# A decoder layer's recurrent sample outputs: from TensorE products with the new state to VectorE sums over a transposed copy of the old state

## The reference

```
S_new = diag(e) S + k^T v        (256 x 512, returned as gla_state_sample)
o     = q S_new                  (512 numbers, goes on into a norm and the branch)
```

## Time and profile before

| | us |
|---|---|
| runs, median of 3 | 5105.1 |
| lowest, highest | 5100.22, 5108.11 |
| profiled execution, its own time | 5101.16 |
| its span, first to last instruction | 5099.3 |
| blocks with units, with TensorE's work alone | 506.15 to 930.45 |
| the 32 blocks after them | 930.45 to 1295.81 |

### The profile page before, as it was taken

The page is one execution under the profiler, slowest core; times in us unless marked ns, Lnnn a source line. Parts: engine busy times, 40 slices in busy tenths (PEclk is TensorE's granted clock), DMA queues, the critical chain, the costliest instruction groups (busy, mean ns, idle before and its releaser), DMA issues.

```text
span 5099.3 us, 63408 instructions
## 1 busy us (share of the span) xinstructions
PE 4302.3 (84%) x24722; PEld 3722.8 (73%) x24722; DVE 3047.0 (60%) x4037; ACT 852.2 (17%) x1238; POOL 1266.2 (25%) x824
## 2 busy tenths in 40 slices
PE   5999999999688989999567568799999999677555
PEld 5998999999676889777456457688788878444222
DVE  5533222211542654675567887778889756698776
ACT  3434333222221233000110000000000000000000
POOL 0000000000000000233123433444434422266665
PEclk9999999999699899999688879899999999888777
DMA  5555555333245455999568879999999998699998
GB/s 178 194 204 179 200 192 206 134 113 113 73 176 218 141 190 192 424 423 420 204 238 363 325 312 411 411 423 423 423 392 400 424 405 354 252 401 382 422 421 362
DMA packets 312222, 1494.07 MB, mean 293 GB/s; under 512 B 34658, under 2 KB 119954, under 8 KB 147132
## 3 DMA queue, kind: packets, MB, share of 16 engines
q0 software_dynamic: 114288, 830.54, 39.6%
q1 hardware_dynamic: 197748, 661.07, 34.3%
HBM read 1411.79 MB, written 79.70 MB: 292 GB/s over the span
## 4 chain that ended last, share of the span: by engine, by line
PE 52%; DMA 26%; DVE 9%; issue 5%; DVEq 3%; POOL 2%; ACT 2%; SPq 0%; POOLq 0%; ACTq 0%
PE psum L501 27%; DMA sb_raw<-in_wstream 15%; PE psum L2500 10%; DMA sb_ring<-in_peer_v,sb_idx_all 8%; PE psum L555 6%; DVE sb_acc L2341 2%; POOL sb_ring L2315 2%; DMA sb_gt<-dram_z 2%; PE psum L2742 2%; DVE sb_acc_b L2643 1%; PE psum L716 1%; PE psum L2724 1%; DVE sb_split L485 1%; PE psum L1127 1%; DVEq L1678 1%
## 5 line engine op out<-in xcount | busy, mean ns | idle before, releaser
L501 PE MATMUL psum<-sb_actr,sb_split 128*128 128x264 f32 x8112 | 1014.3, 287 | 43.9 <-DVE sb_split L485 17.9
L485 DVE TENSOR_TENSOR sb_split<-sb_raw,sb_split 128x2048 fp32r<-128x2048 f32 x201 | 460.8, 2293 | 966.7 <-ACT sb_split L481 965.8
L501 PEld LDWEIGHTS psum<-sb_actr,sb_split 128*128 128x128 f32 x8112 | 1001.4, 191 | 47.6 <-issue 44.0
L2336 DVE CUSTOM_DVE_ANT_0 sb_ring<-sb_ring,sb_htok 128x2048 f32<-128x2048 f32 x264 | 598.3, 2291 | 204.3 <-DMA sb_ring<-in_peer_u,sb_idx_all 189.4
L2226 POOL DMA_INDIRECT sb_ring<-in_peer_u,sb_idx_all x256 | 374.9, 1465 | 1335.8 <-DVE sb_dots L2336 678.1
L2341 DVE SCALAR_TENSOR_TENSOR sb_acc<-sb_ring,sb_coef,sb_acc 128x2048 f32<-128x2048 f32 x256 | 601.9, 2351 | 141.1 <-DMA sb_ring<-in_peer_v,sb_idx_all 125.5
L2226 POOL DMA_INDIRECT sb_ring<-in_peer_v,sb_idx_all x256 | 417.8, 1632 | 664.1 <-DVE sb_acc L2341 556.3
L2742 PE MATMUL psum<-sb_ring,sb_diag 128*128 128x512 f32 x512 | 349.0, 845 | 238.5 <-DMA sb_ring<-in_peer_v,sb_idx_all 231.5
L2643 DVE SCALAR_TENSOR_TENSOR sb_acc_b<-sb_ring,sb_coef_b,sb_acc_b 128x2048 f32<-128x2048 f32 x192 | 451.4, 2351 | 131.0 <-DMA sb_ring<-in_peer_v,sb_idx_all 116.6
L2315 POOL DMA_INDIRECT sb_ring<-in_peer_v,sb_idx_all x256 | 436.5, 1705 | 299.3 <-DVE sb_acc_b L2643 131.5
L2500 PE MATMUL psum<-sb_h2b,sb_raw 128*128 128x256 f32 x2048 | 455.5, 382 | 18.5 <-DMA sb_raw<-in_wstream 18.5
(11 more groups left out here) (366 smaller groups left out, 4274.8 us busy)
## 6 DMA issues: line engine op xcount, KB each, us to landing
sb_raw<-in_wstream SPq DMA_DIRECT2D x386, 1024.0 KB
sb_raw_u<-in_wstream SPq DMA_DIRECT2D x64, 1024.0 KB
dram_z<-sb_zst SPq DMA_DIRECT2D x64, 260.0 KB
sb_states<-in_state SPq DMA_DIRECT2D x32, 512.0 KB, 3.4
out_gla_s<-sb_states SPq DMA_DIRECT2D x32, 512.0 KB, 2.9
sb_vrow<-dram_v SPq DMA_DIRECT2D x8, 1024.0 KB, 5.2
sb_cache<-in_kcache SPq DMA_DIRECT2D x8, 1024.0 KB, 11.5
sb_cache<-in_vcache SPq DMA_DIRECT2D x8, 1024.0 KB, 7.6
```

Source lines behind the costliest of these rows:

```text
L485: nc.vector.tensor_tensor(split[:, slot, 1, :], raw[:, slot, :], split[:, slot, 0, :], ALU.subtract).then_inc(lo_ready, 1)
L501: last = nc.tensor.matmul(psum[:, bank, 0:ntok], w[a], acts(b, kt), start=(i == 0 and a == 0 and b == 0), stop=(i == len(kts) - 1 and a == 1))
L2336: nc.vector.tensor_tensor_reduce(u[:], u[:], htok[:], 1.0, 0.0, ALU.mult, ALU.add, out).then_inc(row_used, 1)
```

## The change

The products of the new state with q are no longer computed. Instead the kernel takes `o = (q * e) S + (q . k) v`:

- A second input array holds each old state transposed, as 128 x 4 x 256 floats per unit (512 KB). SP loads it into one of two new buffers beside the state.
- VectorE does four fused multiply-and-sum operations per unit, each 128 x 256: a piece of the transposed old state times the row q * e, spread over all partitions, summed into one column (`dve_unit`). After a sample's last head it copies the 16 columns into `os_`.
- The rows q * e are made once: VectorE multiplies (`dve_samples_products`, at block N_R + 4), TensorE turns them and sums q * k over the partitions (`pe_samples_q`, at N_R + 8), ScalarE copies them out, SP stores them to DRAM and spreads sample 0's row; the row of the next sample is loaded with its value row.
- The term (q . k) v is made once for all (`dve_samples_own`) and added after the last unit (`dve_samples_done`).
- The units start 12 blocks later, at N_U0 = N_R + 12, and ride with the 32 blocks from there, 20 blocks before the stage ends. The 12 blocks before them are three segments of four.
- TensorE's loop in those blocks is now `seg_loop`, without `pe_unit`; ScalarE has no `act_unit_out`.
- Semaphores are merged and renamed (`v_tok` into `rows_tok`, `keep_made`, `peer_made`, `qm_zeroed` into `pool_made`, `packed` into `unpacked`), with counts adapted.

```diff
+N_U0 = N_R + 12
+N_UNITS = N_U0 + 4 * TS
...
         def sp_samples_start(sp):
 
-            sp.dma_start(states[0][:], state_of(ins["state"], 0, 0)).then_inc(st_in[0], 16)
-            sp.dma_start(states[1][:], state_of(ins["state"], 0, 1)).then_inc(st_in[1], 16)
-            sp.wait_ge(v_tok, 2)
+            for h in range(2):
+                sp.dma_start(states[h][:], state_of(ins["state"], 0, h)).then_inc(st_in[h], 16)
+                sp.dma_start(states_t[h][:], ins["stateT"][h]).then_inc(st_in[h], 16)
+            sp.wait_ge(rows_tok, 2)
...
+        def sp_samples_q(sp):
+
+            sp.wait_ge(rows_tok, 3)
+            sp.dma_start(q_dram[:], q8[:]).then_inc(samples_loaded, 16)
+            sp.wait_ge(samples_loaded, 80)
+            sp.dma_start(qrow[:], row_of(q_dram, 0)).then_inc(vrow_loaded, 16)
...
         def sp_unit(sp, n, s, h, last):
-            unit = n - N_R
+            unit = n - N_U0
             sp.wait_ge(st_done, unit + 1)
             sp.dma_start(state_of(outs["gla_s"], s, h), states[h % 2][:]).then_inc(st_out[h % 2], 16)
+            sp.wait_ge(st_read, unit + 1)
             if h == HEADS - 1 and not last:
-                sp.dma_start(vrow[:], row_of(s + 1)).then_inc(vrow_loaded, 16)
+                sp.dma_start(vrow[:], row_of(v_dram, s + 1)).then_inc(vrow_loaded, 16)
+                sp.dma_start(qrow[:], row_of(q_dram, s + 1)).then_inc(vrow_loaded, 16)
             if h < 2 or not last:
...
+                k = bass.ds(s * HEADS + (h + 2), 1)
+                sp.dma_start(states_t[h % 2][:], ins["stateT"][k].rearrange("a p j d -> p (a j) d")).then_inc(st_in[h % 2], 16)
+                src = ins["state"].rearrange("s h k v -> (s h) k v")[k].rearrange("a (k p) v -> p (a k) v", p=P)
                 sp.wait_ge(st_out[h % 2], s * 32 + 16 * (h // 2 + 1))
-                sp.wait_ge(st_read, unit + 1)
                 sp.dma_start(states[h % 2][:], src).then_inc(st_in[h % 2], 16)
...
+        def act_samples_q(act):
+            act.wait_ge(rows_turned, 3)
+            nc.scalar.activation(q8[:].rearrange("s (b f) -> s b f", b=2), psum[0:TS, 4:6, :], ACT.Copy).then_inc(rows_tok, 1)
...
-        def act_unit_out(act, n, s, h):
-            act.wait_ge(st_read, n - N_R + 1)
-            nc.scalar.activation(os_[:, 4 * h:4 * h + 4, bass.ds(s, 1)], psum[:, 4 + h % 2, 0:4].unsqueeze(2),
-                                 ACT.Copy).then_inc(os_read, 1)
...
+        def dve_samples_products(dve):
+
+            dve.wait_ge(es_ready, 1)
+            nc.vector.tensor_tensor(qes[:], qs[:], es[:], ALU.mult)
+            nc.vector.tensor_tensor(qks[:], qs[:], ks[:], ALU.mult)
+            dve.drain().then_inc(qes_ready, 1)
+
+        def dve_samples_own(dve):
+
+            dve.wait_ge(rows_turned, 3)
+            nc.vector.tensor_reduce(qk[:], psum[:, 6, 0:64].rearrange("p (h d s) -> p h s d", h=HEADS, d=2), AX.X, ALU.add)
+            dve.drain()
+            nc.vector.tensor_tensor(qkv[:].rearrange("p (h j) s -> p h j s", h=HEADS), vs[:].rearrange("p (h j) s -> p h j s", h=HEADS),
+                                    qk[:].unsqueeze(2).to_broadcast([P, HEADS, 4, TS]), ALU.mult)
+
+        def dve_samples_done(dve):
+            dve.drain()
+            nc.vector.tensor_tensor(os_[:], os_[:], qkv[:], ALU.add).then_inc(os_ready, 1)
...
             last.then_inc(st_done, 1)
+            dve.wait_ge(st_in[h % 2], s * 64 + 32 * (h // 2 + 1))
+            for j in range(4):
+                st = states_t[h % 2][:, j, :]
+                last = nc.vector.tensor_tensor_reduce(st, st, qrow[:, h * DK:(h + 1) * DK], 1.0, 0.0, ALU.mult, ALU.add,
+                                                      os_cur[:, 4 * h + j, :])
+            last.then_inc(st_read, 1)
+            if h == HEADS - 1:
+                dve.drain()
+                nc.vector.tensor_copy(os_[:, :, bass.ds(s, 1)], os_cur[:])
...
-        def pe_unit(pe, n, s, h):
-
-            pe.wait_ge(st_done, n - N_R + 1)
-            pe.wait_ge(os_read, n - N_R + 1)
-            for j in range(4):
-                for dt in range(2):
-                    last = nc.tensor.matmul(psum[:, 4 + h % 2, j:j + 1], states[h % 2][:, dt, j * P:(j + 1) * P],
-                                            qs[:, 2 * h + dt, bass.ds(s, 1)], start=(dt == 0), stop=(dt == 1))
-            last.then_inc(st_read, 1)
-
+        def pe_samples_q(pe):
+            pe.wait_ge(qes_ready, 1)
+            pe.wait_ge(rows_tok, 2)
+            for f in range(8):
+                nc.tensor.transpose(psum[0:TS, 4 + f // 4, (f % 4) * P:(f % 4 + 1) * P], qes[:, f, :], ident[:])
+            nc.tensor.matmul(psum[:, 6, 0:64], ones[:], qks[:].rearrange("p f s -> p (f s)"), start=True,
+                             stop=True).then_inc(rows_turned, 1)
...
         def act_gla(act, g):
             if g.samples:
+                act.wait_ge(os_ready, 1)
```

More of the change, by code:

```diff
@@ L69 @@
 N_END = N_WQ + 16
-N_UNITS = N_R + 4 * TS
+N_U0 = N_R + 12
+N_UNITS = N_U0 + 4 * TS
 N_UEND = N_END + NU
@@ L197, in mixer_kernel @@
         vrow = sb("vrow", [P, D], F32, R_M + 41472)
+        states_t = [sb(f"states_t{i}", [P, 4, DK], F32, R_M + 49664 + 4096 * i) for i in range(2)]
+        qrow = sb("qrow", [P, 1024], F32, R_M + 57856)
+        q8 = sb("q8", [TS, 1024], F32, R_M + 66048)
         v8 = sb("v8", [TS, D], F32, R_M + 86528)
@@ L208, in mixer_kernel @@
         low_s = sb("low_s", [RANK, TS], F32, R_SM + 2944)
+        qes = sb("qes", [P, 8, TS], F32, R_P + 66560)
+        qks = sb("qks", [P, 8, TS], F32, R_P + 66816)
+        qk = sb("qk", [P, HEADS, TS], F32, R_P + 67072)
+        qkv = sb("qkv", [P, KT, TS], F32, R_P + 67200)
+        os_cur = sb("os_cur", [P, KT, 1], F32, R_P + 67712)
         ks_cur = sb("ks_cur", [P, 8, 1], F32, R_SM + 2976)
@@ L414, in mixer_kernel @@
         vrow_loaded = sem("vrow_loaded")
-        os_read = sem("os_read")
+        es_ready = sem("es_ready")
+        qes_ready = sem("qes_ready")
+        os_ready = sem("os_ready")
         samples_loaded = sem("samples_loaded")
@@ L580, in unit_loop @@
         def unit_loop(eng, n0, n1, body):
-            assert (n0 - N_R) % 4 == 0 and (n1 - n0) % 4 == 0
+            assert (n0 - N_U0) % 4 == 0 and (n1 - n0) % 4 == 0
             with eng.Fori(0, (n1 - n0) // 4) as i:
@@ L585, in unit_loop @@
                     n = n0 + h
-                    body(i * 4 + n, n % 2, i * 2 + (n - n % 2) // 2, i + (n0 - N_R) // 4, h)
+                    body(i * 4 + n, n % 2, i * 2 + (n - n % 2) // 2, i + (n0 - N_U0) // 4, h)
         def with_units(n0):
-            return N_R <= n0 < N_UNITS
+            return N_U0 <= n0 < N_UNITS
         def sp_samples_first(sp):
@@ L642, in act_samples_start @@
                 if b == 1:
-                    last.then_inc(v_tok, 1)
-                    act.wait_ge(v_turned, 2)
-            last.then_inc(v_tok, 1)
+                    last.then_inc(rows_tok, 1)
+                    act.wait_ge(rows_turned, 2)
+            last.then_inc(rows_tok, 1)
             act.wait_ge(gx_ready, 2)
             nc.scalar.activation(es[:], gxs[:], ACT.Exp, scale=1.0 / GATE_NORM)
-            act.drain()
-            act.sem_inc(os_read, 2)
+            act.drain().then_inc(es_ready, 1)
+        def act_samples_q(act):
+            act.wait_ge(rows_turned, 3)
+            nc.scalar.activation(q8[:].rearrange("s (b f) -> s b f", b=2), psum[0:TS, 4:6, :], ACT.Copy).then_inc(rows_tok, 1)
         def act_unit(act, n, s, h):
-            unit = n - N_R
             if h == 0:
@@ L685, in dve_unit @@
                 dve.drain()
-                dve.wait_ge(vrow_loaded, s * 16 + 16)
-            dve.wait_ge(st_scaled, n - N_R + 1)
+                dve.wait_ge(vrow_loaded, s * 32 + 32)
+            dve.wait_ge(st_scaled, n - N_U0 + 1)
             for dt in range(2):
@@ L747, in sp_project @@
                     sp_samples_start(sp)
+                if n0 == N_R + 8:
+                    sp_samples_q(sp)
                 def body(n, slot, u, ntok=ntok):
@@ L804, in act_project @@
                     act_samples_start(act)
+                if n0 == N_R + 8:
+                    act_samples_q(act)
                 def body(n, slot, u, s=None, h=None, func=func, ntok=ntok, n0=n0):
@@ L921, in dve_project @@
                         dve_samples_first(dve)
+                    if n0 == N_R:
+                        dve_samples_start(dve)
+                    if n0 == N_R + 4:
+                        dve_samples_products(dve)
+                    if n0 == N_R + 8:
+                        dve_samples_own(dve)
+                    if n0 == N_UNITS:
+                        dve_samples_done(dve)
                     seg_loop(dve, n0, n1, lambda n, slot, u: split_lo(dve, n + 1, 1 - slot))
@@ L964, in pe_project @@
                     pe_samples_turn(pe, 0)
-                if with_units(n0):
-                    if n0 == N_R:
-                        pe_samples_turn(pe, 1)
-                        pe.wait_ge(act_lo, 9)
```

(20 more changed lines are left out.)

72 lines of the change are left out of this document (33 added, 39 removed).

## The result

| | before | after |
|---|---|---|
| median of the first set, 4 runs each | 5102.86 | 5043.81 |
| lowest, highest | 5100.22, 5108.11 | 5042.18, 5046.64 |
| profiled execution | 5101.16 | 5042.81 |
| its span | 5099.3 | 5041.1 |

The ratio is 0.9884, with a 95% interval of 0.9866 to 0.9901. The changed kernel is 59.05 us faster by these medians; 55.3 us was forecast. The same kernel in two later sets, each against the kernel before on the same chip, gave 0.9892 (0.9876 to 0.9909) and 0.9889 (0.9872 to 0.9905), which is 55.7 and 56.3 us.

What follows compares the result with a forecast made beforehand. TensorE's work was taken to bound the units' blocks. Removing 57.5 us and adding 2.2 gave -55.3, so 5105.1 became 5049.8, say 5050 us, with a range of 5044 to 5062.

Steps and rivals of the forecast that it cites:

- What bounds the kernel: Blocks N_R to N_UNITS - 1: TensorE's work sets the pace, 13.21 us a round, with the products on the path in full.
- Removed, 57.5 us: 32 units' rounds fall from 13.21 to 11.42 us; 53.8 if the extra 0.12 us a block stays.
- third rival: Products cheaper than their place in the chain, only 0.4 of 1.68 us truly theirs: gain 14.4, 5091 us; chance 0.01.
- Added on TensorE, 2.2 us: At N_R + 8: eight transposes and one float32 matmul 2.1 us, switch 0.1, on the path; bounds 1.05 and 8.3.
- The sums on VectorE, 0.42 with 0.08 for the read: Four sums over 128 x 256 per unit, 0.50 us each with the read, 2.0 together, hidden in 11.42 us blocks.
- second rival: VectorE becomes the bound if a short sum costs 2.37 us: round 13.2, 5107 us, no change; chance 0.02.
- Transfers: Units' stage: DMA work 7.4 us per block, 12.5 at a last head, mean 8.7 of 11.42, 76%; weights land in time.
- 4 us of margin: At a sample's last head: weights land 13 to 15 us into the block and may land at 18.6 or so.
- the first and the last rival: Weights late at a sample's last head, 5074, chance 0.05; transfers bounding the stage for good, 5115 or more, chance 0.02.
- Behind the stage, nothing given back: Stage behind N_BA starts about 55 us earlier, near 1241; later work follows in sequence, so the gain reaches the end.

Runs made afterwards that it cites:

- gate-later version: Kernel after, with the second half of the values turned into two other PSUM banks and the samples' gate at N_R + 4 instead of N_R: 5037.10 us, ratio 0.9871.

## Why the prediction was right or wrong

The forecast was 5050 us with a range of 5044 to 5062; the first set gave 5043.81, just below the range, and the later two 5047.1 and 5048.5, inside it. Two things of the sum failed: the term for the new step on TensorE was twice what it measured, and the scatter of the stages behind was taken too small. By steps:

- **What bounds the kernel.** Right. TensorE's work set the pace from N_R to N_BA, and the 56.2 us are all in that stretch.
- **Removed, 57.5 us.** Right, the choice of 57.5 over 53.8 included: blocks with units fell to 11.41 us at a DMA share of 0.75, and one product that needs nothing brought the extra 0.1 us back. The price of 105 ns a pass held in rows of products: twenty-four passes take 2.57 us and thirty-two 3.46, so the third rival, cheaper products, fell. A product that stands alone took less, 0.12 us for two passes. That the stationary piece makes the price was argued and not shown: no run separates the weight load from the product. The floor of about 25 ns that the Trainium skill states in "TensorE: Matmul & The Clock Gate", section "Wait — 56ns, not 53.3ns?", was reached by none of these products.
- **Added on TensorE, 2.2 us: the term that was mis-sized.** It measured 0.87 + 0.17 = 1.04. I priced a transpose by L707 at 504.29 us, 0.23 each. That row stands right behind the pause of 4.9 us and ran at the lower granted clock, which I had used in the same paragraph for the block behind it and not for the row itself. The gate-later version shows the same eight at that very place at 0.87 us once the pause is gone. Windows of the eight transposes, before and in that version (the clock is the third number from the end):

```profile
504.29:506.15 1.86, 1.86 (x9) 1.26 (x10) 0.00 (x0) 0.00 (x0) 0.00 (x0) 0.50 0.36 138
...
500.57:501.45 0.88, 0.88 (x11) 0.75 (x9) 0.00 (x0) 0.76 (x2) 0.00 (x0) 1.00 0.00 0
```

A transpose at full clock is 0.11 us. With it the sum is 57.5 - 1.04 = 56.5, against 56.2 measured in the stretch, 55.7 and 56.3 in the later medians.
- **The sums on VectorE, 0.42 with 0.08 for the read.** Measured 418 and 80 ns; side by side they cost 0.35 each, so four are 1.4 and not 2.0 us. Hidden, as said. The second rival, VectorE as the bound, needs more than four times as many sums.
- **Transfers.** The DMA share came out at 0.75 (0.76 said). The 4 us of margin was too small an account: two more loads of 512 KB per unit cost TensorE 1.0 us. Weights did come late, ScalarE waited for them ten times and up to 3.5 us, but within the cover. Nothing in the runs speaks for the first and the last rival, which I gave 0.07 together.
- **Behind the stage, nothing given back.** Right within the scatter of 10 us, and there the range was too narrow. My lower end was 5105.1 - 56.45 - 4.88 = 5043.77, which I rounded to 5044; it allowed for the small price of the transposes and for the runs of the kernel before, but for no scatter of the kernel after. I took the median shown, 5105.1, as the base, with the 4.9 us by which one of its three runs lay below it. One more run of the kernel before moved that median by 2.2 us, and the first set of the changed kernel lay low. Of the 6.2 us between 5050 and 5043.81, 1.2 are the transposes and 2.2 the base; the other 2.8 (0.2 of it rounding) are less than the 10 us by which the stages behind differ between profiles of the same kernel; no run gives them another cause.

## What to carry to other kernels

Before a duration is borrowed from a row, look at what stood before that row and at its granted clock: eight transposes took 1.86 us behind a pause and 0.87 without it. Work that overlaps on an engine is priced by the distance of two starts, not by the length of one row. And where an effect lies in one steady stretch, measure it there: the stretch repeated within 0.3 us in three profiles of the kernel after (within 1.3 us, if the variants whose additions were hidden are counted), the whole kernel only within 10.

## What the runs showed of the hardware that was not expected

TensorE's granted clock can fall while the profile shows it busy without a gap. Behind 3.46 us of matmuls with one moving column, in 23 of 32 rounds, and behind 2.57 us of them in 10 of 32, the block of 96 matmuls took 13.05 us or more instead of 11.54; where its windows were read, the lower level (0.50 in a window of 2 us) lasted some 3 us. Behind the 1.68 us of the kernel before, no such block is seen between 519.16 and 928.77, with a clock of 1.00 over all of it. So the products that the change removed were worth 57.5 us, but doubling them cost 92.4 us, of which only 57 were their own time: 1.6 times that.
